# Cache attention: the four pages of a ring slot in four column groups of the array, added up by a selecting matmul

## The reference, cut to what matters

```python
s_past = jnp.einsum('bqhcd,bshcd->bhcqs', q, k_past, preferred_element_type=jnp.float32) * scale
w = diff_combine(jnp.concatenate([s_past, s_new], axis=-1), lam).astype(v_new.dtype)
return (jnp.einsum('bhqs,bshe->bqhe', w[..., :P], v_past)
        + jnp.einsum('bhqs,bshe->bqhe', w[..., P:], v_new))
```

## Time and profile before

| | |
|---|---|
| median of 3 runs | 1536.25 us (1536.1 to 1543.18) |
| span of the profiled execution | 1536.8 us |
| TensorE matmul busy | 1397.7 us (91%) |
| TensorE weight load busy | 968.0 us (63%) |
| VectorE busy | 856.5 us (56%) |
| ScalarE busy | 534.2 us (35%) |
| cache attention's values (L756), busy | 127.9 us in 256 records |
| last chain, share by engine | TensorE 77%, VectorE 15% |

### The profile page before, as it was taken

One profiled execution on the slowest core, in us unless ns is written; L12 is line 12 of the kernel. 1 busy time (PEld: TensorE's weight loads), 2 busy tenths in 40 slices (PEclk: granted clock), 3 DMA queues, 4 the chain that ended last, 5 costly groups with the idle time before them and its releaser, 6 DMA issues.

```text
span 1536.8 us, 19072 instructions
## 1 busy us (share of the span) xinstructions
PE 1397.7 (91%) x7054; PEld 968.0 (63%) x7054; DVE 856.5 (56%) x1097; ACT 534.2 (35%) x613; POOL 21.2 (1%) x26
## 2 busy tenths in 40 slices
PE   5999899999999988999877898888898999999986
PEld 1583735788888885498322222228355888888864
DVE  1435463666666622554797999655705666656434
ACT  0331213555555512343111111123215555555321
POOL 2000010000000000000000000000100000000000
PEclk9999999999999998999877788798857999999988
DMA  9927440899999874354438987865104999999400
GB/s 337 365 92 266 165 164 0 294 342 341 335 337 337 307 286 154 125 184 153 151 109 314 328 314 273 314 226 195 60 0 163 341 336 343 341 339 339 149 2 28
DMA packets 143712, 355.36 MB, mean 231 GB/s; under 512 B 4706, under 2 KB 4899, under 8 KB 143652
## 3 DMA queue, kind: packets, MB, share of 16 engines
q1 hardware_dynamic: 142388, 350.97, 63.9%
q0 software_dynamic: 1264, 3.59, 0.7%
HBM read 351.27 MB, written 3.28 MB: 231 GB/s over the span
## 4 chain that ended last, share of the span: by engine, by line
PE 77%; DVE 15%; issue 3%; ACT 2%; DMA 1%; SPq 0%; ACTq 0%; POOL 0%; DVEq 0%
PE pj L372 27%; PE gu L590 23%; PE pj L609 15%; DVE wring L1763 4%; PE pj L756 3%; DVE tokB L1766 3%; PE tb L403 3%; PE tb L406 3%; PE gu L438 3%; PE pj L383 1%; DMA wring<-in_ada_w 1%; DVE xT L1435 1%; DVE yT L1433 1%; DVE rs L1432 1%; ACT reg L1069 1%
## 5 line engine op out<-in xcount | busy, mean ns | idle before, releaser
L1618 DVE TENSOR_TENSOR wlo<-wring,whi 128x2048 fp32r<-128x2048 f32 x128 | 290.1, 2288 | 102.2 <-ACT whi L1173 102.1
L1173 ACT ACTIVATE whi<-wring 128x2048 fp32r<-128x2048 f32 x128 | 245.0, 1918 | 140.4 <-PE gu L590 140.4
L609 PEld LDWEIGHTS pj<-tokB,wring 128*128 128x128 f32 x2048 | 233.5, 192 | 4.7 <-issue 2.1
L609 PE MATMUL pj<-tokB,wring 128*128 128x128 f32 x2048 | 234.0, 275 | 1.7 <-issue 1.7
L590 PE MATMUL gu<-whi,xhi 128*128 128x512 f32 x512 | 205.9, 402 | 13.2 <-DVE xlo L1644 13.2
L1069 ACT ACTIVATE reg<-pj 128x264 f32<-128x264 f32 (+4 forms) x166 | 83.2, 507 | 380.0 <-PE pj L372 209.7
L590 PE MATMUL gu<-wlo,xhi 128*128 128x512 f32 x512 | 203.5, 398 | 0.0
L590 PE MATMUL gu<-whi,xlo 128*128 128x512 f32 x512 | 201.9, 394 | 0.0
L372 PE MATMUL pj<-wring,cT 128*9 128x512 f32 x384 | 175.6, 612 | 5.4 <-DMA wring<-in_ada_w 4.6
L756 PE MATMUL pj<-wring,ws 128*8 128x512 f32 x256 | 127.9, 659 | 6.4 <-DMA wring<-in_cache_v 5.4
L590 PEld LDWEIGHTS gu<-whi,xhi 128*128 128x128 f32 x512 | 98.1, 192 | 35.0 <-DVE xlo L1644 8.2
(11 more groups left out here) (281 smaller groups left out, 1652.1 us busy)
## 6 DMA issues: line engine op xcount, KB each, us to landing
wring<-in_moe_w_gate SPq DMA_DIRECT2D x32, 2048.0 KB, 9.5
wring<-in_moe_w_up SPq DMA_DIRECT2D x32, 2048.0 KB, 10.3
wring<-in_moe_w_down SPq DMA_DIRECT2D x32, 2048.0 KB, 9.9
wring<-in_ada_w SPq DMA_DIRECT2D x24, 2048.0 KB, 10.4
wring<-in_cache_k SPq DMA_DIRECT2D x64, 512.0 KB, 5.0
wring<-in_cache_v SPq DMA_DIRECT2D x64, 512.0 KB, 4.9
wring<-in_a_w_in SPq DMA_DIRECT2D x4, 2048.0 KB, 19.8
wring<-in_a_w_out SPq DMA_DIRECT2D x2, 2048.0 KB, 15.3
```

Of the source, the lines that this page charges most:

```text
L609: m = pe.matmul(bank[:, i * P:(i + 1) * P], w[:, k, f * P:(f + 1) * P], aT[:, k, :], start=(k == 0), stop=(k == FB - 1))
L1173: act.activation(whi[q], quarter(wring, q, s), ACT.Copy).then_inc(hi_ready, 1)
L1618: dve.tensor_tensor(quarter(wlo, q, s), quarter(wring, q, s), whi[q].bitcast(F32), ALU.subtract).then_inc(lo_ready, 1)
```

## The change

In `values` the four pages p of a slot write to partitions 32p to 32p+31 of the bank, so each uses its own group of 32 columns of the array. The weights are padded from 8 to 32 columns with zeros, which are set once (`memset`); `sW` holds two sequences in turns in place of all eight. Each bank now holds four partial sums, one a column group, over two pages each. ScalarE copies 128 partitions instead of 8. The row extraction becomes eight matmuls: the 128 x 128 block c of `osb` is the stationary operand, and the moving one is a new constant column that has a one in rows c, 32+c, 64+c and 96+c. So it picks head c and adds the four partial sums at once, and VectorE copies eight columns that lie side by side. To make room, `lgT` of the router lies in `rs`.

```diff
--- before.py
+++ after.py
@@ -69,7 +69,8 @@
 
 
 K_ID, K_ROT, K_ONE, K_TRI, K_MASK, K_IOTA, K_PART = 0, 128, 256, 384, 512, 768, 768 + T
-K_N = 768 + T + 5
+K_SEL = 768 + T + 5
+K_N = 768 + T + 5 + 9
 
 V_LNG, V_LNB, V_AG, V_AB, V_SUB, V_N = 0, 32, 64, 72, 80, 81
 
@@ -91,6 +92,7 @@
     k[:, K_MASK + P:K_MASK + 2 * P] = np.where(
         np.arange(P)[:, None] >= np.arange(P)[None, :], 0.0, NEG)
     k[:, K_PART:K_PART + 5] = np.arange(P)[:, None] + P * np.arange(5)[None, :]
+    k[:, K_SEL:K_SEL + 9] = np.arange(P)[:, None] % 32 == np.arange(9)[None, :]
     return k
 
 
@@ -188,7 +190,7 @@
         mT = sb("mT", [P, 48, NR])
         rs = sb("rs", [P, T])
         epsc = sb("epsc", [P, 1])
-        lgT = sb("lgT", [NE, T])
+        lgT = rs[0:NE, :]
         lg = sb("lg", [P, 3, NE])
         score = sb("score", [P, 3, NE])
         sel = sb("sel", [P, 3, NE])
@@ -269,7 +271,7 @@
         crow = crows[0:NR, :]
         psc = mrows[:, :].rearrange("p (j c s) -> p j c s", j=2, c=2)
         pex = crows[:, :].rearrange("p (j c s) -> p j c s", j=2, c=2)
-        sW = wsT[:, 0:4, :].rearrange("p a (x g h) -> p (a x) g h", g=NPG, h=H)
+        sW = wsT[:, 0:4, :].rearrange("p a (x h) -> p (a x) h", h=32).rearrange("p (i g) h -> p i g h", i=2)
         pwT = wsT[:, 4:8, :].rearrange("p (j t) q -> p j t q", j=2)
         lamv = lamx[0:1, :, :]
         smx = lamx[:, 2:4, :].rearrange("p a d -> p (a d)")
@@ -751,10 +753,10 @@
                 for n in range(2):
                     if k == 0:
                         pe.wait_ge(pj_evac, g.n + n + 1 - NBANK)
-                    out = pj[(banks[0] + n) % NBANK][0:H, :]
+                    bank = pj[(banks[0] + n) % NBANK]
                     for p in range(4):
-                        m = pe.matmul(out, sW[:, s, 4 * k + p, :], wring[:, slot, p * D + n * 512:p * D + (n + 1) * 512],
-                                      start=(k == 0 and p == 0), stop=(k == 1 and p == 3))
+                        m = pe.matmul(bank[32 * p:32 * p + 32, :], sW[:, s % 2, 4 * k + p, :],
+                                      wring[:, slot, p * D + n * 512:p * D + (n + 1) * 512], start=(k == 0), stop=(k == 1))
                     if k:
                         m.then_inc(pj_done, 1)
                 if k:
@@ -816,7 +818,7 @@
                 if s >= 2:
 
                     pe.wait_ge(pj_evac, at[f"values{s - 2}"])
-                    small([((P, H * c, H), tr(osb[0:H, c * P:(c + 1) * P], H)) for c in range(C)])
+                    small([((P, c, 1), mm(osb[:, c * P:(c + 1) * P], kst[:, K_SEL + c:K_SEL + c + 1])) for c in range(C)])
                     at[f"rows{s - 2}"] = b.n
                 if s < 3:
                     ada_turn(1, 6 + s)
@@ -1295,7 +1297,7 @@
 
                         act.wait_ge(tb_done, at[f"rows{s - 3}"])
                     for n in range(2):
-                        evac(osb[0:H, n * 512:(n + 1) * 512], rows=H, n=512)
+                        evac_wide(osb[:, n * 512:(n + 1) * 512], P)
                 if s == NB + 1:
                     tile_split()
                 if s == 0:
@@ -1749,6 +1751,7 @@
             dve.wait_ge(stored["kp"], 16)
 
             dve.tensor_copy(sS[:, :, NPG, :], snew)
+            link(dve.memset(wsT[:, 0:4, :], 0.0))
 
             def scores(s, k, q):
 
@@ -1838,7 +1841,7 @@
                     link(dve.tensor_scalar(odd, odd, nlam[:, 0:1], None, ALU.mult))
                     link(dve.tensor_tensor(sS[:, m], sS[:, m], wide, ALU.mult))
                     e4 = sS[:, m].rearrange("p g (h c) -> p g h c", c=2)
-                    dve.tensor_tensor(sW[:, m], e4[:, 0:NPG, :, 0], e4[:, 0:NPG, :, 1], ALU.add)
+                    dve.tensor_tensor(sW[:, m % 2, :, 0:H], e4[:, 0:NPG, :, 0], e4[:, 0:NPG, :, 1], ALU.add)
                     ready(dve.tensor_tensor(wnew[:, m, :], e4[:, NPG, :, 0], e4[:, NPG, :, 1], ALU.add))
                 if s == NB + 1:
                     tile_split()
@@ -1849,7 +1852,7 @@
                 if s >= 2:
 
                     empty(dve.tensor_copy(hT[:, :, TP + s - 2:TP + s - 1],
-                                          batch()[:, 0:(H + 1) * (H - 1) + 1:H + 1].unsqueeze(2)))
+                                          batch()[:, 0:H].unsqueeze(2)))
                 if s < 3:
                     mod_rows(1, 6 + s)
                 if s < NB:
```

## The result

| | before | changed |
|---|---|---|
| median | 1539.34 us (5 runs, 1536.10 to 1543.18) | 1547.19 us (5 runs, 1543.62 to 1552.46) |
| ratio | | 1.0065, 95% interval 1.0041 to 1.0090 |
| span of the profiled execution | 1536.8 us | 1550.7 us |
| mean granted clock | 0.921 | 0.887 |

By the ratio the change costs about 10 us (6 to 14); the two medians lie 7.9 us apart. The forecast was 1541, +5.3. Ten more runs of the unaltered changed kernel (`after_again`) gave 1.0057 (1.0037 to 1.0076).

A forecast was written before the change was run, and what follows sets the result against it. VectorE was taken to set turns s=3 to s=7 of the attention. Terms -5.1 + 16.3 - 5.3 + 0.4 - 1.0 = +5.3 us on 1536.25 gave about 1541 us, range 1530 to 1548.

The forecast's parts named there:

- A change too small to resolve: Whole kernel: time within the 0.5% bound, 1528.6 to 1543.9 us; chance 0.49.
- everything outside the attention at nothing: Stages outside the cache attention: no term in the sum, and stages behind it keep their length.
- What bounds the turns: Turns s=3 to s=7: VectorE sets them, so a shorter L756 buys nothing; a longer extraction costs one for one.
- The price of the extraction: Row extraction, s=2 to s=7: +3.0 us at half clock in five turns, +1.3 at full in one.
- the idles of s=2: Turn s=2: VectorE's waits of 3.21 and 1.90 us behind the values both go, -5.1 us.
- Six extractions on VectorE's path: Turns s=2 to s=7: every extraction delays VectorE's row copy and the next scores, +16.3 us together.
- Column groups, at most two at a time: Values matmuls: two records overlap, so sixteen last about 3.9 us at full clock instead of 7.03.
- four at once: Rival, attention: four column groups run together, TensorE idler and at low clock; +10.3, 1546.5 us; chance 0.14.
- the extraction in s=9: Turn s=9: extraction at full clock after unbroken work, +0.4 us; +2.0 at half clock.
- no concurrency: Rival, values matmuls: column groups run one after another, s=2 and s=8 gains vanish; +9.7, 1546 us; chance 0.22.
- The nine extra constants lie beside longer work: Constants added for the extraction: hidden beside longer work, no cost in the sum.
- The +1.7 us for a start at half clock: Turn s=8: ada tile slowed by low clock, some 1.7 us, counted only in four at once.

The follow-up runs named there:

- groups_only: Changed kernel with the old extraction of eight transposes, leaving out three of the four column groups' partial sums; ratio 0.9960 to the kernel before.
- layout: Kernel before with only nine more constants and lgT placed in rs; ratio 1.0010.
- after_place: Changed kernel with its nine selecting columns in a tile of their own, so tiles ahead of the router keep their former addresses; ratio 1.0064 to the kernel before.
- layout64: Kernel before with nine constants, lgT in rs and eight more unused constants, moving later tiles by 64 bytes; ratio 1.0036.
- early_ada: Changed kernel with row extraction earlier in both queues, eight unused constants, and s=8's ada load ahead of the last value pages; ratio 0.9944 to the kernel before.
- early_ada_place: early_ada with the addresses of the kernel before; 1521.57 us, ratio 0.9901 to the kernel before.
- place_a: after_place, unaltered, profiled a second time; attention 290.1 us.
- place_b: after_place, unaltered, profiled a third time; attention 289.9 us.

## Why the prediction came out as it did

The sign of the sum and the mechanism in the attention held; the size was off by nearly half: +5.3 forecast, about +10 measured, and 1547 lies at the very top of the range. A change too small to resolve had been given the higher chance (0.49), slower 0.39. The step that failed is the one that put everything outside the attention at nothing; inside it, where +5.3 was forecast and +3.8 to +5.2 measured, two errors of place and count cancel in part, which is luck.

- **What bounds the turns**: right. 74 us less of L756 made turns s=3 to s=6 no shorter; groups_only, with the old extraction, shows it (28.81 against 28.28).
- **The price of the extraction**: right in kind, small in count. 3.5 us at half clock, 1.9 at full; but all six ran at half clock, not five, and behind them the first scores came 0.17 us late. The table gives -2.0 + 12.0 + 2.9 = 12.9 us up to s=8, the idles of s=2 included, where the prediction had 16.3 - 5.1 = 11.2.
- **Six extractions on VectorE's path**: this was an error of place. The one in s=7 does not reach the end: in s=8 everything waits for the ada tile's load. What releases SyncE's queue is VectorE's last key reduction, which ends at 1001.7, ahead of that extraction; four page loads go first, and the ada tile's is issued at 1006.9 and lands 10.1 us later:

```profile
999.42 2.29 DVE L1769 TENSOR_REDUCE tokB<-wring 128x32 f32<-128x2048 f32 x1
...
1003.49 3.55 PE L408 MATMUL tb<-kst,ws 128*128 128x1 f32 x16 [0.43 <-DVE hT L1850]
```

  The reduction to the issue takes 5.2 us, as it did before (984.0 to 989.2), so the extraction does not delay it. So s=7 loses 2.9 us and s=8 gains 8.3, not 5.3. I had added a delay and a load that lie side by side.
- **Column groups, at most two at a time**: wrong, without consequence for the turns, which VectorE sets either way; at most it is why six extractions and not five ran at half clock. The window in s=8 of the changed kernel counts eight records in one microsecond at half clock, that of the kernel before two:

```profile
1011.00:1012.00 1.00, 1.00 (x8) 0.20 (x4) 0.00 (x0) 0.78 (x1) 0.00 (x0) 0.50 1.02 387
```

```profile
827.00:828.00 1.00, 1.00 (x2) 0.14 (x1) 1.00 (x1) 0.00 (x0) 0.00 (x0) 0.50 0.86 279
```

  (each counts the records that touch it). Sixteen records in 3.64 us at half clock, where one streams for 0.85, are four at once. The rival *four at once* had that right and its total, 1546.5, is near the measured one, but again by luck: of its terms only the six slow extractions came in every profiled execution, the extraction in s=9 took 1.9 to 2.1 us, not 3.6, and the slow ada tile came in two of five; the attention was +3.8 to +5.2, not +10.3. The rival *no concurrency* also said 1546, and its mechanism did not occur. The Trainium skill ("TensorE: Matmul & The Clock Gate", Measured speedup vs the span model) gives 2.38 times for three column tiles; the trace goes further with four. The rule under "The mechanism" on the same page of the Trainium skill, that weight loads pass running matmuls only where their row groups differ, does not agree with this trace: all four groups have all 128 rows, and they ran four at once.
- **"The nine extra constants lie beside longer work"**: this is the term of that step which the runs name. It was put at nothing without a row for it. The constants move every later tile by 32 bytes, and 32 experts take 0.10 us longer each: +3.2 us, shown in the expert's length by layout and taken back there by after_place. In the total it is too small to be seen alone (layout 1.0010, after_place 1.0064 against the changed kernel's 1.0057); twice of it is seen, in layout64 and between early_ada and early_ada_place. Nothing in the trace of before gave a hint of it.
- **The ada tile**: the +1.7 us for a start at half clock, which I had given to a rival alone, occurs in place_a and place_b, two of five profiled executions, not in the first one.
- **Slips in the sums**: in *no concurrency* one of six extractions at half clock adds 1.7 to 7.8, which is 9.5 and not 9.3; with +1.4 for every extraction the sum is -2.6 and not about -2; and the transposes of the kernel before start 0.06 us apart, not 0.05. None moves the forecast.

With the attention at +3.8 to +5.2 and the addresses at +3.2, 7 to 8.4 of about 9 to 10 us are accounted for in the changed kernel. The rest, 1 to 3 us, is as large as the scatter of the parts outside the attention, and stays open. after_place has no part from the addresses, and there 5.2 us of attention stand against a ratio of 10 us (6 to 14): up to 5 us of it are unexplained.

## What to carry to other kernels

Shortening an engine that is not the bound is worth only what stands still for it, here two places of ten turns; and the price is paid where the two engines hand over, so a step that an edit makes longer should go where the bounding engine has other work (3.53 us of waiting became 0.17). Before adding up delays to the end, look for a load that was issued ahead of them: what it hides isn't paid. And keep every tile's address when an edit adds a few columns, or measure the move alone: here it cost 3.2 us, beside 3.8 to 5.2 from the edit itself.

## What the runs showed of the hardware

- Four column groups of fp32 matmuls stream side by side: sixteen records of 512 columns took 3.64 us at half clock; one after another, in one column group, sixteen took 7.03 at full clock.
- With the shorter values TensorE was granted less clock over the attention, 0.59 instead of 0.80 (900 to 1000 us), and work that is still on the path (records that load 128 columns of weights and stream one, 0.11 us each at full clock, 0.21 at half) then took nearly twice as long.
- The gate and up matmuls (512 moving columns, single records) take 11.00, 11.10, 11.21, 11.13 and 11.00 us for 48 with their tiles moved by 0, 32, 64, 128 and 512 bytes; the down matmuls don't react.
